# RWKV systems of direction two transposed, one batch for both directions, scan offset four, and a preparation with unscaled rate sums

## The reference

```
tmat = lax.linalg.triangular_solve(eye + lmat, eye, left_side=True, lower=True, unit_diagonal=True)
v_new = u_i - wk_i @ state
o_i   = q_i @ state + attn_i @ v_new
state = state * exp(gl_i) + einsum('bhcd,bhce->bhde', k_i, v_new)
```

```
w_log = -softplus(-(w0 + tanh(wd) @ w_up)) - 0.5
decay = exp(-exp(w_log))
a     = sigmoid(a0 + ad @ a_up)
k_dir = k * (1 + (a - 1) * k_a)
sa    = -einsum('bhvk,bhk->bhv', state, kk_t)
state = state * w_t + sa * b_t + v_t * k_t        # b = kk * a
o_t   = einsum('bhvk,bhk->bhv', state, r_t)
```

## Time and profile before

| | us |
|---|---|
| median of 3 runs (lowest, highest) | 3989.17 (3984.30, 3995.16) |
| span of the profiled execution | 3990.6 |
| PE busy | 3488.3 (87%) |
| DVE busy | 2133.2 (53%) |
| POOL busy | 791.3 (20%) |
| ACT busy | 662.1 (17%) |
| `rwkv_prep`, 2821.8 to 3232.4 | 410.6 |
| `scans` up to the first step with both scans, 3232.4 to 3420.2 | 187.8 |
| 12 steps from there, to 3722.4 | 302.2 |
| rest of `scans` and `closing`, to 3990.6 | 268.2 |

### The profile page before, as it was taken

One profiled execution on the slowest core, in us unless ns is written; L12 is line 12 of the kernel. 1 busy time (PEld: TensorE's weight loads), 2 busy tenths in 40 slices (PEclk: granted clock), 3 DMA queues, 4 the chain that ended last, 5 costly groups with the idle time before them and its releaser, 6 DMA issues. The chain is left out here.

```text
span 3990.6 us, 64126 instructions
## 1 busy us (share of the span) xinstructions
PE 3488.3 (87%) x28192; PEld 2775.3 (70%) x28192; DVE 2133.2 (53%) x2308; ACT 662.1 (17%) x1079; POOL 791.3 (20%) x817
## 2 busy tenths in 40 slices
PE   6999999999998989799999999999567645677798
PEld 3777777777887878688888888876355535676376
DVE  2477777743334555544453353339688835332564
ACT  2122222212000001211110010012233301221100
POOL 0111111111000000034005125000574789000000
PEclk8999999999999999899999999998689867888799
DMA  9444444444332453322232222328478698777243
GB/s 398 143 155 145 163 149 148 151 166 166 119 119 98 176 188 132 114 91 88 84 111 90 85 103 105 125 108 301 130 197 217 165 231 169 180 227 205 69 175 106
DMA packets 359077, 607.72 MB, mean 152 GB/s; under 512 B 136440, under 2 KB 244080, under 8 KB 330128
## 3 DMA queue, kind: packets, MB, share of 16 engines
q1 hardware_dynamic: 305488, 472.23, 37.6%
q0 software_dynamic: 21712, 92.42, 7.1%
q10 hardware_dynamic: 31600, 38.99, 2.8%
HBM read 469.17 MB, written 134.39 MB: 151 GB/s over the span
## 5 line engine op out<-in xcount | busy, mean ns | idle before, releaser
L182 PE MATMUL front_ps<-b_hT,p_wb 128*128 128x512 f32 x4224 | 979.7, 392 | 6.8 <-PEq L94 6.8
L182 PEld LDWEIGHTS front_ps<-b_hT,p_wb 128*128 128x128 f32 x4224 | 790.0, 188 | 187.5 <-issue 20.6
L1772 PE MATMUL in_ps<-b_hT,in_wb 128*128 128x512 f32 (+1 forms) x3264 | 749.7, 390 | 13.4 <-DVE in_wb L1759 13.4
L1772 PEld LDWEIGHTS in_ps<-b_hT,in_wb 128*128 128x128 f32 (+1 forms) x3264 | 606.7, 187 | 147.5 <-DVE in_wb L1759 13.6
L1757 DVE CAST in_wb<-in_raw 128x2048 fp32r<-128x2048 f32 (+1 forms) x68 | 82.7, 1216 | 535.4 <-PE in_ps L1772 530.5
L170 DVE CAST p_wb<-p_raw 128x2048 fp32r<-128x2048 f32 x88 | 108.0, 1227 | 430.5 <-PE front_ps L182 420.2
L813 POOL DMA_DIRECT2D front_mwb<-in_w_ada x128 | 101.3, 796 | 794.8 <-PE front_mps L823 790.0
L1772 PEld LDWEIGHTS in_ps<-b_hc,in_wb 128*128 128x128 f32 (+1 forms) x1728 | 211.4, 189 | 3.2
L1772 PE MATMUL in_ps<-b_hc,in_wb 128*128 128x256 f32 (+1 forms) x1728 | 212.7, 283 | 0.0
L172 DVE TENSOR_TENSOR p_wb<-p_raw,p_wb 128x2048 fp32r<-128x2048 f32 x88 | 201.8, 2293 | 3.0
L1211 PE MATMUL mid_ps<-mid_wb,b_hT 128*128 128x512 f32 x768 | 178.6, 393 | 13.4 <-DVE mid_wb L1196 13.4
(11 more groups left out here) (456 smaller groups left out, 4347.6 us busy)
## 6 DMA issues: line engine op xcount, KB each, us to landing
p_raw<-in_w_in_tiles SPq DMA_DIRECT2D x88, 1024.0 KB, 6.1
in_raw<-in_w_in_tiles SPq DMA_DIRECT2D x67, 1024.0 KB, 4.8
front_mwb<-in_w_ada POOLq DMA_DIRECT2D x128, 512.0 KB, 5.0
open_wb<-in_w_ada_groups SPq DMA_DIRECT2D x32, 1024.0 KB, 11.3
g_scr<-gprep_ob SPq DMA_DIRECT2D x8, 3474.0 KB, 11.6
merge_raw<-in_w_branch_units SPq DMA_DIRECT2D x32, 512.0 KB, 4.6
mid_raw<-in_w_o_parts SPq DMA_DIRECT2D x32, 512.0 KB, 3.7
last_raw<-in_w_out_parts SPq DMA_DIRECT2D x32, 512.0 KB, 3.7
```

The lines of the kernel that those rows point to most:

```text
L182: last = self.nc.tensor.matmul(self.ps[:, n % 2, :], self.wb[:, n % 2, x, kt, :], self.hT[:, y, kt, :], start=kt == term == 0, stop=kt == ...
L1772: last = self.nc.tensor.matmul(self.ps[0:width, n % 3, first:end], self.wb[:, n % 2, x, kt, 0:width], h[:, y, kt, :], start=kt == term == ...
```

## The change

1. **Layout.** `systems` keeps only the 96 delta systems of each direction. The RWKV systems get an array of their own, `r_systems`, by pair, direction, head of the pair and chunk, with rows of W = 96 columns: an image of 64x96, in which columns 32 to 95 hold the system and columns 0 to 31 are free for a result.
2. **Direction two transposed.** Its product of operands is computed with the factors changed round (`turned_products`), and masked with the other triangle, so that both directions are lower systems of one form.
3. **Batches.** `solve_pairs` takes two pairs with both directions, 96 systems. It reads only columns 32 to 95 into the image, uses the free corner of the image as its temporary, makes three flipped copies instead of two, and writes the whole image back. POOL does the two delta batches and three of the four pair batches in `rwkv_prep`, each as soon as its own two pairs are stored, and the fourth in `scans`. The split inside a batch and the reading ahead by SP are gone.
4. **Scans.** LAG is 4, so the loop has 16 steps, eight of which hold both scans; from n = 12 on a step folds two tiles (`FOLDS`). The inverses of RWKV are read with 96 columns. The outputs of a delta step are computed after its values in the banks `work[0]` and `work[1]`, both groups in a row, and the state update waits until ACT has taken them. The clearing of blocks on POOL waits for the load alone, and no longer for PE's `middle`.
5. **Preparation.** `add_up` is a single scan for each direction (over a reversed view for direction two) of the plain sigmoids; the factor exp(-0.5) goes into the scale of the exponentials. `gx` is gone: the sums without the token itself are the same exponentials shifted by one token, with an edge column copied. The first part of `kd` moves to ACT (`direct`, an Identity with scale and bias); `ks` is formed once a pair.

```
+W = C + HC
+WIDE = HC * W + HC
+def solve_pairs(nc, pool, link, m, r_systems, batch, before):
+    pool.dma_start(full[:, :, HC:W], images_of(r_systems, batch).rearrange("p (i j) -> p i j", j=W)[:, :, HC:W]).then_inc(m.n_in, 16)
+    pool.wait_ge(m.n_in, before * 16 + 16)
+    link(ops.memset(m.diagonal, 2.0))
+    for j in range(HC - 1):
+        na, ni = j + 1, HC - 1 - j
+        a, after = slice(0, na), slice(na, HC)
+        t = full[:, HC:HC + na, 0:C].rearrange("p a (b y) -> p b a y", b=2)[:, :, :, 0:ni]
+        link(ops.tensor_tensor(t, y[:, :, a, j:j + 1].to_broadcast([BATCH, 2, na, ni]),
+                               y[:, :, j:j + 1, after].to_broadcast([BATCH, 2, na, ni]), ALU.mult))
+        link(ops.tensor_tensor(y[:, :, a, after], y[:, :, a, after], t, ALU.subtract))
...
+    link(ops.tensor_copy(full[:, lo, first], flip(full[:, lo, middle])))
+    link(ops.tensor_copy(full[:, hi, first], flip(full[:, lo, last])))
+    link(ops.tensor_copy(full[:, hi, middle], flip(full[:, hi, last])))
...
+    pool.dma_start(images_of(r_systems, batch), m.image).then_inc(m.y_out, 16)
...
     def add_up(self, dve, i, d):
+        order = (lambda x: x[:, ::-1]) if d else (lambda x: x)
-        self.link(self.nc.vector.tensor_scalar(swd, swd, -math.exp(-0.5), None, ALU.mult))
-        self.link(self.nc.vector.tensor_tensor_scan(gd, self.reset[:], swd, 0.0, ALU.mult, ALU.add))
-        if d == 0:
-            self.tt(gxd, gd, swd, ALU.subtract)
-        else:
-            whole = chunks(gd)[:, :, C - 1:C].to_broadcast([P, NCH, C])
-            self.tt(chunks(gxd), whole, chunks(gd), ALU.subtract)
-            self.tt(gd, gxd, swd, ALU.add)
+        self.link(self.nc.vector.tensor_tensor_scan(order(self.g[:, d]), self.reset[:], order(self.sw[:, d]), 0.0, ALU.mult, ALU.add))
...
+    def turned_products(self, pe, i):
...
+                self.nc.tensor.matmul(self.ps_m[r, c * P:c * P + C], ob[r, c, self.AR:self.AR + C], b[r, at], start=True, stop=True)
...
+                last = self.nc.tensor.matmul(self.ps_m[r, c * P + C:(c + 1) * P], b[r, at], ob[r, c, self.AR + C:self.AR + P], start=True, stop=True)
...
-                for n, (batch, d) in enumerate(((0, 0), (0, 1), (1, 0), (1, 1))):
+                for batch in range(RP // PAIRS - 1):
+                    for u in range(3):
+                        pool.wait_ge(m.stored[u], m.STORED * len(range(u, 2 * PAIRS * (batch + 1), 3)))
+                    pool.wait_ge(solver.y_out, 16 * (batch + 2))
+                    solve_pairs(nc, pool, link, solver, r_systems, batch, batch + 2)
...
-            if g == 1:
-                self.state_outputs(pe, k, g)
-            self.value_outputs(pe, k, g)
+            pe.wait_ge(self.s["o_out"], 4 * (k - NCC) + 2 * g + 2)
...
-LAG = 8
+LAG = 4
+FOLDS = GH // LAG
...
-                sp.dma_start(second.rows, rows_of(systems, 2, 0)).then_inc(second.n_in, 16)
-                sp.wait_ge(first.y_out, 64)
-                sp.dma_start(first.rows, rows_of(systems, 2, 1)).then_inc(first.again, 16)
...
+                before.finish(pool)
+                solve_pairs(nc, pool, Link(pool, second.chain), second, r_systems, RP // PAIRS - 1, 0)
```

More of the change, by code:

```diff
@@ L2653, in turn, with rows_of, solve @@
     link(ops.tensor_copy(full[:, near, far], flip(full[:, near, near])))
[L2656 to L2665, removed]
+def rows_of(systems, d):
+    return systems[d]
+def solve(nc, pool, link, m, systems, d, before):
+    pool.dma_start(m.rows, rows_of(systems, d)).then_inc(m.n_in, 16)
     pool.wait_ge(m.n_in, before * 16 + 16)
-    substitute(nc.gpsimd, link, m, d, range(0, SPLIT))
@@ L2670, in end, with images_of @@
-def end(nc, pool, link, m, systems, batch, d):
-    substitute(nc.gpsimd, link, m, d, range(SPLIT, HC - 1))
+    substitute(nc.gpsimd, link, m, d)
     turn(pool, nc.gpsimd, link, m, d)
     pool.sem_inc(m.tick, 1)
-    pool.dma_start(rows_of(systems, batch, d), m.rows).then_inc(m.y_out, 16)
+    pool.dma_start(rows_of(systems, d), m.rows).then_inc(m.y_out, 16)
+PAIRS = 2
+def images_of(r_systems, batch):
+    return r_systems[PAIRS * batch:PAIRS * (batch + 1)].rearrange("q d h c s x -> (q d h c) (s x)")
@@ L2789, in start @@
         dve.wait_ge(self.given.loaded, 16 * 6)
+        link(nc.vector.tensor_scalar(self.rest[:], self.vec[:, 5], -1.0, 1.0, ALU.mult, ALU.add))
+        dve.sem_inc(self.s["rest_ok"], 1)
     def clear(self, dve, before):
@@ L3436, in middle @@
                 for h in range(2):
[L3437 to L3439 removed]
+                    own, other = quarter(h, d)[0:2]
+                    first, last_cols = self.inv[other, k % 3, d, q, 0:HC], self.inv[other, k % 3, d, q, C:W]
+                    last = self.nc.tensor.matmul(self.px[own, q, :], last_cols if d else first, first if d else last_cols, start=True, stop=True)
         last.then_inc(self.s["mid_ps"], 1)
@@ L3505, in values @@
                 for h in range(2):
-                    last = self.term(self.work[d], q, h, self.inv[:, k % 3, d], self.y[:, d], h, True, True)
+                    last = self.term(self.work[d], q, h, self.inverse(k, d), self.y[:, d], h, True, True)
             last.then_inc(self.s["u_ok"], 1)
@@ L3791, in r_output, with tiles_at, scans @@
         link(nc.vector.tensor_tensor(o, o, self.zr[:, t], ALU.mult))
-LAG = 8
-def scans(nc, k, p2, gain, vectors, bonus, before, given, first, r_scr, v_scr, systems, slots, late, yT):
+LAG = 4
+FOLDS = GH // LAG
+def tiles_at(n):
+    return range(FOLDS * (n - NCH), FOLDS * (n - NCH + 1))
+def scans(nc, k, p2, gain, vectors, bonus, before, given, first, r_scr, v_scr, r_systems, slots, late, yT):
     with Stage(nc, "scan") as st:
@@ L3874, in _ @@
                         r.value_outputs(pe, n - LAG)
+                    if in_g(n) and STEPS[n][2]:
+                        g.outputs(pe, n, 0)
+                        g.outputs(pe, n, 1)
                     if in_g(n):
@@ L3924, in _ @@
                         g.store(act_e, n)
+                    if in_r(n + 1):
+                        r.complete(act_e, n + 1 - LAG)
                     if n >= NCH:
-                        out.take(act_e, n - NCH)
+                        for t in tiles_at(n):
+                            out.take(act_e, t)
                 out.root(act_e)
@@ L3954, in _ @@
                     if n == 0:
-                        r.start(dve)
+                        r.start(dve, before)
                         out.start(dve)
```

218 lines of the change are left out of this document (110 added, 108 removed).

## The result

The changed kernel takes 4090.52 us in the median of 4 runs (4076.85 to 4093.50), the kernel before 3990.28 us on the same chip (3984.30 to 3995.16). The ratio is 1.0242, with a 95% interval of 1.0223 to 1.0262: slower by about 100 us, where 4112 had been forecast. The profiled execution spans 4091.8 us, 101.2 more than the one before.

What follows compares the result with a forecast made beforehand. The end was taken as set by POOL's row of six batches, then 12 scan steps held by SP's loads, then an untouched output part: 3990.6 + 60 + 63 = 4113.6 us, forecast as a 4112 median, range 4010 to 4180.

Steps and rivals of the forecast that it cites:

- The two terms: POOL's row of batches, +60 us to the first shared step, and the 12 scan steps from there, +63 us.
- The row of batches: POOL's six batches: longer reads, solves and write-backs start the first step with both scans at 3480.2, not 3420.2: +60 us.
- the upper end of 40: Each RWKV batch read by POOL: every piece at the mean packet's 79 ns, engines shared at 0.68: 40 us, against 22 taken.
- solves under 72 us in the preparation: POOL's batches in the preparation: solves this short were to show the forecast wrong; 86.6 and 76 us were counted there.
- POOL's relief: Batches beside the preparation: less DVE work could quicken POOL; priced at zero, other end 14 us per batch.
- The twelve steps: From the first step with both scans: eight shared steps instead of four, held by SP's loads, 365 us against 302: +63 us.
- the low end: Twelve steps: eight shared steps at the 26.9 us of the four before (215) and the rest 109: +22 us.
- the first rival: Twelve steps: loads do not hold the shared steps and delta work fills PE's gaps, +22 instead of +63, 4071 us; chance 0.17.
- Part three: Preparation: work removed from DVE may end it up to 60 us earlier; counted as nothing, since its stage ends with batch 5.
- SP keeps up: Shared steps: loads do not hold them and delta work fills PE's gaps, +22 instead of +63, 4071 us; chance 0.17.
- The dear read: RWKV batches: the piecewise read costs its upper end, 18 us more in each of four, +72, 4184 us; chance 0.10.
- the fast POOL: Row of batches: POOL runs ahead, all RWKV batches solve at 72.1 us, step 4 starts near 3376, 3967 us; chance 0.08.

Runs made afterwards that it cites:

- e7_stores: Kernel before with the new preparation arithmetic, POOL waiting ahead of its third batch for seven stores instead of eight: 3964.47 us, ratio 0.9919.

## Why the prediction was right, and where its sizes were off

The sign, the two places and the rough size were right: 4112 forecast, 4090.5 measured, with 123 us forecast as the sum and 101.2 found between the two executions. The two terms were off in opposite directions, by 44 us and 24 us, so that the sum came out nearer than either reason deserved; that part is luck.

**The row of batches: +60 forecast, +15.6 measured.** The structure held (six batches in a row, reads and write-backs between them, the wait of 43.4 us gone, the barrier behind the fifth, PE waiting for the first inverses), and so did the 3029 of the third read (3030 forecast). The prices were too high. The four reads took 16.3, 15.0, 12.1 and 17.4 us from issue to memset, not 22 each: 27 us. The 22 rested on 125 ns for a long packet, which no row shows, and the upper end of 40 does not follow from its own sum (30 us at a share of 0.68 would be 45); the reads stayed below both. Nor were they slow only in the preparation: the fastest had every other engine idle, and the slowest ran beside the scans. The four solves, up to the write-back, took 84.4, 65.8, 64.6 and 67.4 us instead of 86.6, 76, 72.1 and 72.1: 25 us. The 2.6 us for the strided temporary did not appear: in the scan stage the two operations take 862 and 928 ns now, and took 879 to 895 and 952 to 958 before. One sign that was to show the forecast wrong, solves under 72 us in the preparation, thereby came true, and it was this price that was wrong. The write-backs' 13 us held (13.1 and 11.7), though half as much again of 10 is 15. The barrier gave back 11 of this: it cost POOL 12.2 us between write-back and read, where I had put 1. With the landing at 3425.6 (16.5 us behind the write-back instead of 12.5) and 10.2 us from there to the first shared step instead of 15.6, 3480 became 3435.8. The scans began 91 us later and not 125, and the delta steps behind the barrier came to their wait in 62 us, where 86 had been counted, 23 of them one wait for a load before; so PE's wait was 40.2 us, where 21 had been left.

**POOL's relief, forecast at zero with 14 us per batch as the other end.** The substitution of the third batch took 77.3 us with DVE busy 64.0, that of the fourth 59.1 with DVE busy 10.8, that of the fifth 57.9 with every other engine idle, and that of the sixth 60.7 with DVE busy 28.5. The rows stand in the order fifth, sixth, fourth, third:

```profile
3247.50:3305.40 57.90, 0.00 (x0) 0.00 (x0) 0.00 (x0) 0.00 (x0) 52.90 (x63) 0.50 0.00 0
3341.70:3402.40 60.70, 23.96 (x384) 21.42 (x384) 28.48 (x39) 3.00 (x8) 55.71 (x63) 0.64 0.86 182
3158.00:3217.10 59.10, 17.95 (x361) 16.41 (x356) 10.81 (x9) 3.25 (x4) 54.11 (x63) 0.71 0.92 207
3045.60:3122.90 77.30, 56.56 (x906) 46.22 (x905) 63.99 (x50) 29.37 (x32) 72.29 (x63) 0.87 0.80 203
```

So beside a busy DVE the pace was that of the earlier trace rows, as I had argued, and the gain came from DVE being nearly done: its last operation of the preparation ends at 3183.7, inside the fourth batch as I had let it, but with little work left there. For the fifth batch I had taken the pace beside running scans, and it ran beside nothing. The Trainium skill, GPSIMD Engine Reference, section 8. Key points, says that POOL shares its SBUF interfaces with VectorE and contends with some of its instructions. The trace agrees: 18 us between the third batch and the fourth. PE, ACT and the transfers changed between these rows too, so DVE's part in it is not separated.

**The twelve steps: +63 forecast, +87.4 measured.** This is the step of the working that failed, in its reason and in its size: "the shared steps are held by SP". SP's rounds were as long as the steps (31.7 to 41.3 us from the second on), but PE waited for an operand once, 2.3 us. In the twelve steps SP waited 128.5 us for landings, and without these waits the steps grew longer; 66.4 us more it waited for DVE to free buffers. Each delta step beside an RWKV step costs its own matmuls and its share of gaps, 17.5 us (offset 4 against 8 in the changed form) to 19 us (8 against 9 in the other). The rows that should have shown this were in the earlier trace rows: the four shared steps of before held RWKV context steps, which have no outputs, and the 24.3 us of the steps alone held both outputs and folds. Setting 26.9 against 24.3, as the low end and the first rival did for their +22, made a delta step look like 2.6 us. The new order of the delta outputs was to cost nothing, or 1 us a step if SP were not late; PE's waits for DVE ahead of the second half of `keys` made 7.2 us in the eight steps, against 0.7 in four before. Taken from one first RWKV matmul to the next, steps 4 to 6 took 30.1, 33.2 and 31.7 us (25.4 and twice 30.5 forecast), those with outputs of both 36.3, 37.6, 44.4 and 38.8 (36 forecast), and steps 12 to 14 86 us (87 forecast).

**Part three** was mis-sized by the same view: I counted nothing for the preparation, since its stage ends with the fifth batch. That is so in the changed kernel. But by itself this arithmetic gains 27 us, because POOL's wait in the first half of the preparation is real time. What it is worth inside the changed kernel was not run. Measured against it, the rest of the change costs about 125 us.

Of the rivals, "SP keeps up" was right on SP and wrong on the gaps, which the delta work did not fill: they grew. The dear read and the fast POOL did not come.

## What to carry to other kernels

When two interleaved scans share one engine, count what each step puts on that engine, and compare steps of one kind only; work that runs in a wait for someone else is nearly free, and moving it behind that wait costs its matmuls and more (17 to 19 us for each delta step here). A change in several parts should be priced part by part on the chip: here one part gains 27 us by itself, inside a change that loses 100. A wait removed from a long row of dependent work can come back at the next barrier or read, as it did twice here.

## What the runs showed of the hardware that was not expected

- 6144 pieces of 256 bytes with gaps between them landed 12.1 to 17.4 us after their issue, where 96 rows of 16 KB had taken 9.4 to 13.0. The issue itself takes POOL 2.2 us instead of 0.5.
- A strided result in SBUF cost POOL's tensor_tensor nothing (862 ns for the multiplication with a strided result, 879 and 895 before with a packed one, all in the scan stage).
- Letting the operand loads of a step overlap, instead of one landing before the next is issued, cost 20 us in the changed kernel. In the kernel with seven stores before the third batch it cost 26:

> e7_stores and also without the six landing waits on SP in the RWKV operand loads. Chain theory: the twelve steps from the first shared one take some 30 us less than 302, 3915 us. Bytes theory: as e7_stores.

Measured: 3988.57 us, ratio 0.9984 (0.9972 to 0.9996), against 0.9919 with the waits.

- With less operand traffic the granted clock over the same matmuls rose from 0.84 to 0.92 of full speed, and their work fell from 284.5 to 259.9 us.
